# First modulation by pairs of shift and scale, gate and up beside it, angles moved into the feed-forward

## Chip, cores and metric

The kernel runs on one core of a Trainium2 chip. The metric is the time of one execution on the device in microseconds (us), as the median of some runs. Engines: TensorE (PE) multiplies matrices, with its weight loads shown as PEld; VectorE (DVE) and ScalarE (ACT) work elementwise; GpSimd (POOL) and SyncE (SP) here mainly issue loads. Each engine runs its own list of instructions in order and waits on semaphores. SBUF is the memory beside the engines, PSUM the eight banks that PE writes.

## The reference, cut to what matters

Two transformer blocks of two layers each act on x of 256 tokens by 1024 features in f32. What matters here is the very beginning of the first block, for layer 0:

```python
c_act = jax.nn.silu(c)
mod = (c_act @ ada_w[l] + ada_b[l]).reshape(bsz, N_SUB, 3, D_MODEL)[:, :, :, None, :]
h = modulate(x, norm_pre[l, 0], mod[:, 0, 0], mod[:, 0, 1])   # rms_norm(x) * gain * (1 + scale) + shift
x = residual_add(x, swiglu(h, ffn_w_gate[l, 0], ffn_w_up[l, 0], ffn_w_down[l, 0]), norm_post[l, 0], mod[:, 0, 2], 0.5)
```

The comment sums up `modulate` and is not in the code. A swiglu is `(silu(h @ w_gate) * (h @ w_up)) @ w_down` with an inner width of 2816. Much later, the second block turns queries and keys by the cosine and sine of angles made from `positions_2`.

## The kernel before, in words

**Feature-major h.** h is held as eight pieces of 128 features by 256 tokens (`hx`, with a high half `hhi` and a low half `hlo`, since PE multiplies f32 split into two parts). A piece m needs shift m and scale m, each a vector of 128. One "unit" of the modulation is 128 of those numbers: a 128x1024 slice of `ada_w` (512 KB), multiplied by silu(c) and summed along its rows on DVE (`tensor_tensor_reduce`, L2210). Units 0 to 7 are the shifts and 8 to 15 the scales of the first sublayer. They are loaded from SP's queue (L420 to L429) and from ACT's (L1524 to L1528), into buffers that other parts use later (`first_ada`, L384 to L389); the last three go into buffers that the first units have left. DVE takes them in the order 0 to 15 (L2208). Each counts up `first_used`.

**Weights.** All weight matrices pass as tiles of 128x2048 f32 (1 MB) through a ring of three slots `raw`. ACT copies a tile to its high half (`split_high`, L1224, into `whi`), DVE subtracts for the low half (`split_low`, L1811, into `wlo`), and SP loads the slot again when the low half is done (L439). In a feed-forward the tiles come as gate 0, up 0, gate 1, up 1, down 0, gate 2, up 2, down 1 and so on: tile 0 is the first gate, tile 4 the first down, tile 7 the second down.

**The opening.** DVE first makes the angles of the second block from the positions (L2182 to L2206, some fifteen small operations, a cosine part and a sine part); ACT takes their sine (L1533). DVE then runs the sixteen units, with the low half of tile 0 after the sixth. POOL loads x when the load of unit 3 has landed (L2524); ACT makes the sums of squares of x and scales its rows (L1537 to L1547); PE transposes them (`turn_rows`, L643) into banks 6, 7, 0 and 1. When all sixteen units are done, DVE adds bias and norm (`shift_scale`, L1833), ACT writes the pieces (`sublayer_begin`, L1343), DVE makes their low halves (L1930) and counts `h_ready`, and PE multiplies gate piece by piece (`features_fresh`, L863), then up in one go (`features_wide`, L874).

**The feed-forward's step on DVE** (`gate_up`, L2136): low half of the next tile, sum of the two gate banks (L2140), a modulation unit for later sublayers (L1830, from `adat`, which POOL refills as units are used, L2535), low half of the next tile, sum of the up banks (L2144), product with silu and its split (L2147 to L2154), another unit. ACT copies bank parts (L1502, L1507) and makes the silu. PE waits in `gate_up` (L887) for the sums of the chunk before and in `down` (L895) for the tile's low half and for `a_ready`.

`keep_busy` (L638) issues products of constants that nothing uses.

## Time and profile before

| | us |
|---|---|
| median of 3 runs (2280.01 to 2280.69) | 2280.08 |
| the profiled execution | 2280.72 |
| its span | 2279.1 |
| PE busy | 2217.8 (97%) |
| DVE busy | 1625.4 (71%) |
| ACT busy | 1234.0 (54%) |
| bytes moved by DMA | 467.27 MB, mean 205 GB/s |

Times in the views are counted from the start of the span. A row of the timeline names an engine, a line of the kernel, the operation, the tile written and those read, and how many such instructions were merged; in brackets stands how long the engine was idle before it and what released it. A "landing" is the time from the issue of a load to its semaphore.

### The profile page before, as it was taken

To read this page: it belongs to the slowest core of one execution; us is meant where nothing else is said; L and a number is where in the kernel's file an instruction comes from. 1 tells how busy PE (TensorE), PEld (TensorE's weight loads), DVE (VectorE), ACT (ScalarE), POOL (GpSimd) and SP (SyncE) were. 2 spreads that over 40 slices of the span, in tenths; PEclk is the share of its full clock that TensorE was granted. 3 is DMA by queue.
4 is the path that set the end of the run, shared out by engine and by line. 5 is a ranking of instruction groups with operands and counts; after the bars stand their busy time and mean duration, and the time that the engine had idled before them with its cause. 6 is when DMAs were issued, how large, how long until landed. Compare 5 with 4: busy or idle time off the path is not lost.

```text
span 2279.1 us, 37401 instructions
## 1 busy us (share of the span) xinstructions
PE 2217.8 (97%) x14332; PEld 1983.1 (87%) x14332; DVE 1625.4 (71%) x2303; ACT 1234.0 (54%) x1721; POOL 77.0 (3%) x143
## 2 busy tenths in 40 slices
PE   3999999999999999999999999999999999999998
PEld 3888989988888888899988899889888998898887
DVE  7888777677778888777686667656656667566665
ACT  4445567564455446585554465655544556565444
POOL 0100000000000010000000000000000000000000
PEclk9999999999999999999999999999999999999999
DMA  8877564547666875655565546334555464344553
GB/s 344 311 277 266 190 229 163 194 178 282 242 236 244 298 272 189 229 181 199 194 222 193 191 160 212 130 142 157 199 187 189 157 234 139 131 165 176 198 189 111
DMA packets 79506, 467.27 MB, mean 205 GB/s; under 512 B 10080, under 2 KB 10800, under 8 KB 33168
## 3 DMA queue, kind: packets, MB, share of 16 engines
q1 hardware_dynamic: 58480, 389.38, 47.6%
q0 software_dynamic: 19312, 71.74, 8.8%
q10 hardware_dynamic: 1584, 4.36, 0.5%
q8 instruction: 89, 1.46, 0.3%
q14 instruction: 41, 0.34, 0.0%
HBM read 458.56 MB, written 1.05 MB: 202 GB/s over the span
## 4 chain that ended last, share of the span: by engine, by line
PE 90%; ACT 4%; DVE 2%; issue 1%; DMA 1%; ACTq 1%; DVEq 0%
PE ps L855 21%; PE ps L860 11%; PE ps L548 11%; PE ps L525 10%; PE ps L526 10%; PE ps L527 10%; PE ps L554 5%; PE ps L809 3%; PE ps L816 2%; PE ps L685 1%; PE ps L699 1%; PE ps L732 1%; DVE wlo L1815 1%; PE ps L651 1%; DMA raw<-in_ada 1%
## 5 line engine op out<-in xcount | busy, mean ns | idle before, releaser
L1815 DVE TENSOR_TENSOR wlo<-raw,whi 128x2048 fp32r<-128x2048 f32 x360 | 824.0, 2291 | 204.1 <-ACT whi L1231 190.8
L1231 ACT ACTIVATE whi<-raw 128x2048 fp32r<-128x2048 f32 x359 | 686.8, 1914 | 244.1 <-PE ps L527 195.5
L855 PE MATMUL ps<-hx,whi 128*128 128x512 f32 x2112 | 513.8, 391 | 0.1
L855 PEld LDWEIGHTS ps<-hx,whi 128*128 128x128 f32 x2112 | 392.0, 188 | 79.9 <-issue 0.6
L860 PE MATMUL ps<-hx,wlo 128*128 128x256 f32 x2112 | 288.5, 283 | 0.0
L860 PEld LDWEIGHTS ps<-hx,wlo 128*128 128x128 f32 x2112 | 276.8, 191 | 9.8
L548 PE MATMUL ps<-hx,whi 128*128 128x256 f32 x2176 | 276.6, 285 | 3.4 <-ACT set_a L1251 3.4
L548 PEld LDWEIGHTS ps<-hx,whi 128*128 128x128 f32 x2176 | 265.5, 191 | 6.7 <-issue 6.2
L525 PE MATMUL ps<-whi,yhi 128*128 128x512 f32 (+1 forms) x560 | 215.6, 385 | 0.0
L526 PE MATMUL ps<-wlo,yhi 128*128 128x512 f32 (+1 forms) x560 | 215.1, 384 | 0.0
L527 PE MATMUL ps<-whi,ylo 128*128 128x512 f32 (+1 forms) x560 | 214.4, 383 | 0.0
L1502 ACT ACTIVATE set_b<-ps 128x512 f32<-128x512 f32 x66 | 39.6, 600 | 220.8 <-PE ps L860 220.8
L1830 DVE CUSTOM_DVE_ANT_0 adat<-adat,cact 128x1024 f32<-128x1024 f32 x128 | 155.3, 1220 | 3.7 <-DMA adat<-in_ada 3.1
L554 PE MATMUL ps<-hx,wlo 128*128 128x256 f32 x1088 | 141.5, 283 | 0.0
L554 PEld LDWEIGHTS ps<-hx,wlo 128*128 128x128 f32 x1088 | 135.5, 192 | 0.0
L1507 ACT ACTIVATE set_b<-ps 128x512 f32<-128x512 f32 x66 | 39.5, 598 | 155.4 <-PE ps L860 155.4
L527 PEld LDWEIGHTS ps<-whi,ylo 128*128 128x128 f32 x560 | 105.2, 188 | 21.1
L525 PEld LDWEIGHTS ps<-whi,yhi 128*128 128x128 f32 x560 | 105.4, 188 | 18.9
L526 PEld LDWEIGHTS ps<-wlo,yhi 128*128 128x128 f32 x560 | 105.4, 188 | 18.2
L525 PE MATMUL ps<-whi,hx 128*128 128x512 f32 (+1 forms) x320 | 119.7, 374 | 1.3 <-DVE wlo L1815 0.7
L527 PE MATMUL ps<-whi,hx 128*128 128x512 f32 (+1 forms) x320 | 117.9, 368 | 0.0
L526 PE MATMUL ps<-wlo,hx 128*128 128x512 f32 (+1 forms) x320 | 117.8, 368 | 0.0
(281 smaller groups left out, 3002.6 us busy)
## 6 DMA issues: line engine op xcount, KB each, us to landing
raw<-in_w SPq DMA_DIRECT2D x360, 1024.0 KB, 4.9
adat<-in_ada POOLq DMA_DIRECT2D x128, 512.0 KB, 4.7
blk<-in_block POOLq DMA_DIRECT2D x2, 926.5 KB, 7.4
raw<-in_ada SPq DMA_DIRECT2D x3, 512.0 KB, 9.9
set_b<-in_ada SPq DMA_DIRECT2D x3, 512.0 KB, 11.6
raw<-in_ada ACTq DMA_DIRECT2D x3, 512.0 KB, 13.1
set_a<-set_b SPq DMA_DIRECT2D x24, 64.0 KB
x<-in_x POOLq DMA_DIRECT2D x1, 1024.0 KB, 10.2
```

Source lines behind the costliest of these rows:

```text
L525: mm(out_ap, sh, mh, start=start and first, stop=False, skip_group_check=skip)
L526: mm(out_ap, sh, ml, start=False, stop=False, skip_group_check=skip)
L527: last = mm(out_ap, sl, mh, start=False, stop=stop and end, skip_group_check=skip)
L548: mm(ps[:, bank, i * S:(i + 1) * S], whi[:, slot, col:col + P], h[:, k, :], start=(i == 0 and k == 0 and h is hhi), stop=False, skip_group ...
L554: last = mm(ps[:, bank, i * S:(i + 1) * S], wlo[:, slot, col:col + P], hhi[:, k, :], start=False, stop=(k == KD - 1), skip_group_check=True)
L809: mm(out_ap, whi[:, slot, kk * 512 + i * P:kk * 512 + (i + 1) * P], y[:, n % 2, kk, :], start=(i % 2 == 0 and kk == 0 and y is yhi), stop= ...
L816: last = mm(ps[:, bank + i // 2, (i % 2) * S:(i % 2 + 1) * S], wlo[:, slot, kk * 512 + i * P:kk * 512 + (i + 1) * P], yhi[:, n % 2, kk, :] ...
L855: mm(ps[:, bank + i, :].rearrange("p (a s) -> p a s", a=2), whi[:, slot, k * 256 + i * P:k * 256 + (i + 1) * P], hx[:, :, k, :], start=fir ...
L860: return mm(ps[:, bank + i, 0:S], wlo[:, slot, k * 256 + i * P:k * 256 + (i + 1) * P], hhi[:, k, :], start=False, stop=end)
L1231: A(whi[:, slot, :], raw[:, slot, :], ACT.Copy).then_inc(*T.counts("hi_ready"))
L1815: tt(wlo[:, slot, :], raw[:, slot, :], whi[:, slot, :].bitcast(F32), ALU.subtract)\
L1830: nc.vector.tensor_tensor_reduce(adat[:, slot, :], adat[:, slot, :], cact[:, :], 1.0, 0.0, ALU.mult, ALU.add, out_ap).then_inc(*T.counts(" ...
```

## The change

- The units are taken in the order shift 0, scale 0, shift 1, scale 1, and so on (`first_unit`). Their buffers change; three units use `raw` slots 0 and 2, so tile 0 is loaded when four units are used and tile 2 when six are; tile 1 is loaded from ACT's queue among the units. The load of positions goes last. x is loaded when the second unit has landed.
- ACT loads the table for silu ahead of its wait. The squares of x are two operations of 128x1024 in place of four, with one root for both.
- The transposes go to banks 0 to 3. `first_pieces` on ACT makes shift and scale of one piece from its two units (two 128x1 operations), then writes both f32 and high half of that piece; DVE makes the low half (`first_low`), between its units. The high half of tile 1 stands between pieces 3 and 4, DVE's low half of tile 1 after unit 13 of the new order.
- `first_gate_up` on PE multiplies pieces into gate and up side by side as they come.
- DVE's first gate sum stands ahead of the low half of tile 2 (`fresh`).
- The angles are made inside the first feed-forward, one half after each of the first two chunks (`beside`), and their sine on ACT behind the loop (`sines`).

The diff, cut to its core:

```diff
@@ -260,6 +260,7 @@
         H_BANK = (6, 7, 0, 1)
+        FIRST_H_BANK = (0, 1, 2, 3)
...
@@ -381,12 +384,15 @@
-        first_ada = [raw[:, 1 + i // 2, (i % 2) * D:(i % 2 + 1) * D] for i in range(4)]
+        first_ada = [set_a[:, 8:12, :].rearrange("p a s -> p (a s)"), set_a[:, 12:16, :].rearrange("p a s -> p (a s)")]
+        first_ada += [raw[:, j, i * D:(i + 1) * D] for j in (0, 2) for i in range(2)]
         first_ada += [t.rearrange("p a s -> p (a s)") for t in
-                      (set_b[:, 0:4, :], set_b[:, 4:8, :], set_b[:, 8:12, :], set_a[:, 16:20, :],
-                       merged[:, 0:4, :], merged[:, 4:8, :], ff[:, :, :])]
-        first_ada += [adat[:, 0, :], adat[:, 1, :]]
-        first_ada += [first_ada[2], first_ada[3], first_ada[4]]
+                      (set_b[:, 0:4, :], set_b[:, 4:8, :], set_b[:, 8:12, :], set_a[:, 0:4, :], set_a[:, 4:8, :],
+                       set_a[:, 16:20, :], ff[:, :, :])]
+        first_ada += [adat[:, 0, :], adat[:, 1, :], blk[:, 0:D]]
+        def first_unit(i):
+            return i // 2 + 8 * (i % 2)
@@ -418,15 +424,13 @@
             sp.dma_start(cact[:, :], cin.partition_broadcast(P)).then_inc(s_c, 16)
-            sp.dma_start(raw[:, 0, :], w[0]).then_inc(sems["raw_full0"], 16)
-            for i in (2, 4, 6, 8, 10, 12):
-                sp.dma_start(first_ada[i], ada[i]).then_inc(s_first[i], 16)
-            for i in (13, 14, 15):
-                sp.wait_ge(sems["first_used"], i - 10)
-                sp.dma_start(first_ada[i], ada[i]).then_inc(s_first[i], 16)
-            for j, used in ((1, 2), (2, 15)):
-                sp.wait_ge(sems["first_used"], used)
-                sp.dma_start(raw[:, j, :], w[j]).then_inc(sems[f"raw_full{j}"], 16)
+            for i in range(0, 16, 2):
+                if i == 6:
+                    sp.wait_ge(sems["first_used"], 4)
+                    sp.dma_start(raw[:, 0, :], w[0]).then_inc(sems["raw_full0"], 16)
+                sp.dma_start(first_ada[i], ada[first_unit(i)]).then_inc(s_first[i], 16)
+            sp.wait_ge(sems["first_used"], 6)
+            sp.dma_start(raw[:, 2, :], w[2]).then_inc(sems["raw_full2"], 16)
@@ -640,7 +644,7 @@
-            def turn_rows():
+            def turn_rows(banks=H_BANK):
...
@@ -892,6 +896,47 @@
+            def first_gate_up():
+                T.n["g_chunks"] += 1
+                fresh_h[0] = False
+                gate, up = (4, 0), (6, 1)
+                def wides(to, k):
+                    for i in range(2):
+                        wide(*to, k, i, k == 0)
+                def narrows(to, k):
+                    for i in range(2):
+                        last = narrow(*to, k, i, k == KD - 1)
+                    return last
+                pe.wait_ge(*T.nth("hi_ready", 1))
+                for k in range(4):
+                    pe.wait_ge(*T.next("h_ready"))
+                    wides(gate, k)
+                pe.wait_ge(*T.next("lo_ready"))
+                for k in range(4):
+                    narrows(gate, k)
+                pe.wait_ge(*T.nth("hi_ready", 2))
+                for k in range(4):
+                    wides(up, k)
+                pe.wait_ge(*T.next("lo_ready"))
+                for k in range(4):
+                    narrows(up, k)
+                for k in range(4, KD):
+                    pe.wait_ge(*T.next("h_ready"))
+                    wides(gate, k)
+                    last = narrows(gate, k)
+                    if k < 6:
+                        wides(up, k)
+                        narrows(up, k)
+                last.then_inc(*T.counts("tile_used"))
+                for k in range(6, KD):
+                    wides(up, k)
+                    last = narrows(up, k)
+                last.then_inc(*T.counts("tile_used"))
@@ -907,8 +952,11 @@
-            def ffn(gate=None, more=True):
-                gate_up()
+            def ffn(gate=None, more=True, first=False):
+                if first:
+                    first_gate_up()
+                else:
+                    gate_up()
@@ -927,13 +975,12 @@
             pe.wait_ge(s_idle, 1)
-            turn_rows()
-            pe.wait_ge(sems["first_used"], 16)
-            keep_busy(8, 2)
+            turn_rows(FIRST_H_BANK)
+            keep_busy(20, 7)
...
                     fresh_h[0] = True
-                    ffn(0)
+                    ffn(0, first=layer == 0)
@@ -1354,6 +1401,27 @@
+            def first_pieces():
+                T.n["mods_ready"] += 1
+                act.wait_ge(s_base, 1)
+                for m in range(KD):
+                    if m == 4:
+                        act.wait_ge(sems["raw_full1"], 16)
+                        A(whi[:, 1, :], raw[:, 1, :], ACT.Copy).then_inc(sems["hi_ready"], 1)
+                    act.wait_ge(sems["first_used"], 2 * m + 2)
+                    A(modf[:, 0, m:m + 1], modc[:, 0, m:m + 1], ACT.Identity, bias=p1(0, "ada_b", m, 1))
+                    A(modf[:, 0, 8 + m:9 + m], modc[:, 0, 8 + m:9 + m], ACT.Identity,
+                      scale=p1(0, "norm_pre", m, 1), bias=gate_b[:, m:m + 1])
+                    act.drain()
+                    if m % 2 == 0:
+                        act.wait_ge(*T.next("tr_ready"))
+                    src = ps[:, FIRST_H_BANK[m // 2], m % 2 * S:(m % 2 + 1) * S]
+                    for dst in (h32, hhi):
+                        last = A(dst[:, m, :], src, ACT.Identity, scale=modf[:, 0, 8 + m:9 + m],
+                                 bias=modf[:, 0, m:m + 1])
+                    last.then_inc(*T.counts("t2_ready"))
...
@@ -1513,6 +1581,9 @@
                         tile_done(False)
+                if sines:
+                    act.wait_ge(sems["ang_ready"], 1)
+                    A(tables2[:, :, :], tables2[:, :, :], ACT.Sin).then_inc(sems["tab_ready"], 1)
@@ -1521,40 +1592,43 @@
-            act.dma_start(pos_in, posin.partition_broadcast(P)).then_inc(s_pos, 16)
-            act.dma_start(const[:, N_MATRICES:], const_in[:, N_MATRICES:]).then_inc(s_pos, 16)
+            act.dma_start(first_ada[1], ada[first_unit(1)]).then_inc(s_first[1], 16)
+            act.dma_start(first_ada[3], ada[first_unit(3)]).then_inc(s_first[3], 16)
+            act.dma_start(const[:, N_MATRICES:], const_in[:, N_MATRICES:]).then_inc(s_eps, 16)
             act.dma_start(const[:, 0:N_MATRICES], const_in[:, 0:N_MATRICES]).then_inc(s_const, 16)
-            for i in (0, 1, 3, 5, 7, 9, 11):
-                act.dma_start(first_ada[i], ada[i]).then_inc(s_first[i], 16)
-            act.wait_ge(s_pos, 32)
+            act.preload_act_table_set("silu_and_others")
...
             A(cact[:, :], cact[:, :], ACT.Silu).then_inc(*T.counts("c_ready"))
-            act.wait_ge(*T.next("ang_ready"))
-            A(tables2[:, :, :], tables2[:, :, :], ACT.Sin).then_inc(*T.counts("tab_ready"))
+            for i in range(5, 16, 2):
+                if i == 11:
+                    act.dma_start(raw[:, 1, :], w[1]).then_inc(sems["raw_full1"], 16)
+                act.dma_start(first_ada[i], ada[first_unit(i)]).then_inc(s_first[i], 16)
+            act.dma_start(pos_in, posin.partition_broadcast(P)).then_inc(s_pos, 16)
             use_ln_exp()
-            split_high()
+            act.wait_ge(s_eps, 16)
             act.wait_ge(s_x, 16)
-            for t, c_ in ((0, 0), (1, 0), (0, 1), (1, 1)):
-                add_square(x[:, t, side(c_)], t, c_, x_sums)
-                if c_ == 0:
-                    first_half(x_sums, t, 2 + t)
-                if (t, c_) == (0, 1):
-                    row_root(x_sums, 0, 2, r_x, T.counts("x_rms"))
-            row_root(x_sums, 1, 3, r_x, T.counts("x_rms"))
+            act.wait_ge(sems["first_used"], 2)
+            for t in range(2):
+                A(unit_x[:, t, :], x[:, t, :], ACT.Square, accum_out=x_sums[:, t, 0:1])
+            act.drain()
+            A(r_x[:, :], x_sums[:, :, 0], ACT.Ln, bias=c("eps"), scale=1.0 / D)
+            act.drain()
+            A(r_x[:, :], r_x[:, :], ACT.Exp, scale=-0.5)
...
                     .then_inc(*T.counts("u1_ready" if (t, c_) == (1, 0) else "u_ready"))
+            split_high()
...
                 with T.layer(LAYER1):
-                    sublayer_begin(modf[:, 0, 8:16], modf[:, 0, 0:8])
                     if layer == 0:
-                        act.wait_ge(sems["raw_full1"], 16)
-                        A(whi[:, 1, :], raw[:, 1, :], ACT.Copy).then_inc(sems["hi_ready"], 1)
-                    ffn(False)
+                        first_pieces()
+                    else:
+                        sublayer_begin(modf[:, 0, 8:16], modf[:, 0, 0:8])
+                    ffn(False, sines=layer == 0)
...
@@ -2133,11 +2207,14 @@
-                def gate_up(own=None):
+                def gate_up(own=None, fresh=False):
                     v.drain()
-                    tile_done(False)
+                    if not fresh:
+                        tile_done(False)
...
                     tt(gate_sum, gate_sum, ps[:, 4:6, 0:S], ALU.add).then_inc(*T.counts("ga_ready"))
+                    if fresh:
+                        tile_done(False)
@@ -2154,12 +2231,14 @@
-                gate_up(own_gate)
+                gate_up(own_gate, fresh)
...
                 ada(0)
+                beside(0)
...
                 tile_done(False)
+                beside(1)
@@ -2179,14 +2258,18 @@
-            v.wait_ge(s_pos, 32)
             posf, ang, kf = bufA[:, 0, 0:S], bufA[:, 1, 0:S], bufB[:, 0, 0:S]
-            nc.vector.tensor_copy(posf, pos_in[:, :])
-            v.drain()
-            ts(ang, posf, c("invf"), None, ALU.mult)
-            v.drain()
-            for i, quarter in enumerate((0.25, 0.0)):
-                ts(kf, ang, 1.0 / (2 * math.pi), quarter, ALU.mult, ALU.add)
+            def angles(i):
+                if i == 0:
+                    v.wait_ge(s_eps, 16)
+                    v.wait_ge(s_pos, 16)
+                    nc.vector.tensor_copy(posf, pos_in[:, :])
+                    v.drain()
+                    ts(ang, posf, c("invf"), None, ALU.mult)
+                    v.drain()
+                ts(kf, ang, 1.0 / (2 * math.pi), 0.0 if i else 0.25, ALU.mult, ALU.add)
@@ -2203,28 +2286,51 @@
                 last = ts(r, r, -3.1415925, 3.1415925, ALU.max, ALU.min)
-            last.then_inc(*T.counts("ang_ready"))
+                if i == 1:
+                    last.then_inc(sems["ang_ready"], 1)
             v.wait_ge(*T.next("c_ready"))
-            for i in range(16):
-                v.wait_ge(s_first[i], 16)
-                nc.vector.tensor_tensor_reduce(first_ada[i], first_ada[i], cact[:, :], 1.0, 0.0, ALU.mult, ALU.add,
-                                               modc[:, 0, i:i + 1]).then_inc(*T.counts("first_used"))
-                if i == 5:
-                    split_low()
-            T.n["x_rms"] += 2
+            def first(*units):
+                for i in units:
+                    u = first_unit(i)
+                    v.wait_ge(s_first[i], 16)
+                    nc.vector.tensor_tensor_reduce(first_ada[i], first_ada[i], cact[:, :], 1.0, 0.0, ALU.mult, ALU.add,
+                                                   modc[:, 0, u:u + 1]).then_inc(sems["first_used"], 1)
+            def first_low(*pieces):
+                for m in pieces:
+                    v.wait_ge(*T.next("t2_ready"))
+                    tt(hlo[:, m, :], h32[:, m, :], hhi[:, m, :].bitcast(F32), ALU.subtract)\
+                        .then_inc(*T.counts("h_ready"))
+            first(0, 1)
+            v.wait_ge(s_load, 16 * N_LOADS)
+            stt(out=gate_b[:, 0:8], in0=p1(0, "ada_b", 8, 8), scalar=1.0, in1=p1(0, "norm_pre", 0, 8),
+                op0=ALU.add, op1=ALU.mult).then_inc(s_base, 1)
+            first(2, 3, 4, 5, 6, 7, 8, 9)
+            split_low()
             T.n["u_ready"] += 3
-            v.wait_ge(s_load, 16 * N_LOADS)
...
                     if layer == 0:
-                        shift_scale(0, 0)
                         new_gain()
-                    sublayer_begin()
+                        first_low(0)
+                        first(10, 11)
+                        first_low(1, 2, 3)
+                        first(12, 13)
+                        split_low()
+                        first_low(4, 5)
+                        first(14, 15)
+                        first_low(6, 7)
+                    else:
+                        sublayer_begin()
                     ts(gate_b[:, 0:24], p1(layer, "b_gate"), 0.5, None, ALU.mult)
-                    ffn(ada_units=3, after=lambda: (gate_of(layer, 0, 0.5), new_gate(), shift_scale(layer, 1), new_gain()))
+                    ffn(ada_units=3, after=lambda: (gate_of(layer, 0, 0.5), new_gate(), shift_scale(layer, 1), new_gain()),
+                        beside=angles if layer == 0 else lambda i: None, fresh=layer == 0)
...
@@ -2521,7 +2627,7 @@
             g.dma_start(norms2_all[:, :], norms2_in[:, 0:16 * DEPTH]).then_inc(s_load, 16)
-            g.wait_ge(s_first[3], 16)
+            g.wait_ge(s_first[1], 16)
```

## Rows read from the trace of the kernel before

**Rows 1.** The page's slices of the span: busy tenths of PE and of DVE.
```profile
PE   3999999999999999999999999999999999999998
...
DVE  7888777677778888777686667656656667566665
```

**Rows 2.** Timeline of PE: start us, us, engine, line, operation, count [idle before].
```profile
34.80 3.65 PE L651 MATMUL ps<-const,set_a 128*128 128x128 f32 x16 [34.80 <-ACT set_a L1546]
38.10 2.05 PE L641 MATMUL ps<-idle 128*128 128x256 f32 x8
39.95 0.75 PE L855 MATMUL ps<-hx,whi 128*128 128x512 f32 x1
...
40.71 0.41 PE L855 MATMUL ps<-hx,whi 128*128 128x512 f32 x1
...
51.51 3.82 PE L855 MATMUL ps<-hx,whi 128*128 128x512 f32 x16
...
62.64 0.40 PE L525 MATMUL ps<-whi,yhi 128*128 128x512 f32 x1
...
79.22 0.40 PE L525 MATMUL ps<-whi,yhi 128*128 128x512 f32 x1
```

**Rows 3.** Windows: length, busy PE, PEld, DVE, ACT, POOL, granted clock, DMA.
```profile
50.00:60.00 10.00, 10.00 (x59) 8.86 (x59) 8.98 (x14) 6.28 (x6) 1.06 (x2) 1.00 0.92 349
```

**Rows 4.** Timeline of DVE in the opening.
```profile
9.10 0.29 DVE L2184 CAST bufA<-bufC 128x256 f32<-128x256 int32 x1 [9.10 <-DMA const<-in_const]
...
12.74 0.29 DVE L2189 TENSOR_SCALAR bufB<-bufA 128x256 f32<-128x256 f32 x1
...
15.61 1.22 DVE L2210 CUSTOM_DVE_ANT_0 raw<-raw,cact 128x1024 f32<-128x1024 f32 x1
...
35.43 1.22 DVE L2210 CUSTOM_DVE_ANT_0 raw<-raw,cact 128x1024 f32<-128x1024 f32 x1
...
36.58 1.22 DVE L2210 CUSTOM_DVE_ANT_0 set_b<-set_b,cact 128x1024 f32<-128x1024 f32 x1
...
43.55 0.43 DVE L1943 TENSOR_TENSOR hx<-merged,hx 128x256 fp32r<-128x256 f32 x1 [0.28 <-ACT hx L1354]
```

**Rows 5.** Timeline of DVE in the first feed-forward.
```profile
50.02 0.68 DVE L2140 TENSOR_TENSOR set_b<-set_b,ps 128x512 f32<-128x512 f32 x1
...
60.15 2.29 DVE L1815 TENSOR_TENSOR wlo<-raw,whi 128x2048 fp32r<-128x2048 f32 x1
62.36 0.68 DVE L2140 TENSOR_TENSOR set_b<-set_b,ps 128x512 f32<-128x512 f32 x1
...
74.33 2.29 DVE L1815 TENSOR_TENSOR wlo<-raw,whi 128x2048 fp32r<-128x2048 f32 x1 [0.38 <-issue]
```

**Rows 6.** DMA view of 0 to 60: GB/s in forty slices of 1.5 us.
```profile
GB/s 0 157 255 380 383 391 414 407 421 404 407 418 404 412 412 415 423 404 407 404 432 429 257 5 0 197 431 431 401 412 418 428 83 393 410 399 382 229 371 259
```

**Rows 7.** DMA view of 23 to 26 by queue (POOL's q0, ACT's q10): packets, MB.
```profile
q0 software_dynamic: 78, 0.64, 52.9%
...
q10 hardware_dynamic: 73, 0.29, 23.6%
```

**Rows 8.** DMA issues at 19.1, 36.7 and 38.1: size, us to landing.
```profile
x<-in_x POOLq DMA_DIRECT2D x1, 1024.0 KB, 10.2
...
raw<-in_w SPq DMA_DIRECT2D x1, 1024.0 KB, 4.8
...
adat<-in_ada POOLq DMA_DIRECT2D x1, 512.0 KB, 7.1
```

**Rows 9.** Timeline of ACT.
```profile
30.08 0.29 ACT L1292 ACTIVATE part<-x_sums,const 128x1 f32<-128x1 f32 x1
...
42.90 0.62 ACT L1354 ACTIVATE hx<-ps,modf 128x256 fp32r<-128x256 f32 x1
...
46.96 0.65 ACT L1502 ACTIVATE set_b<-ps 128x512 f32<-128x512 f32 x1
```

**Rows 10.** Timeline of PE, 1501 to 1503: its longest wait after the opening.
```profile
1501.98 1.19 PE L548 MATMUL ps<-hx,whi 128*128 128x256 f32 x8 [1.71 <-ACT set_a L1251]
```

More of the change, by code:

```diff
@@ L291, in build @@
         s_c = ctx.enter_context(nc.semaphore("s_c"))
+        s_eps = ctx.enter_context(nc.semaphore("s_eps"))
+        s_base = ctx.enter_context(nc.semaphore("s_base"))
         s_idle = ctx.enter_context(nc.semaphore("s_idle"))
@@ L650, in turn_rows @@
                             at = (m % 2) * S + t * P
-                            last = nc.tensor.transpose(ps[:, H_BANK[m // 2], at:at + P],
+                            last = nc.tensor.transpose(ps[:, banks[m // 2], at:at + P],
                                                        unit_x[:, t, m * P:(m + 1) * P], ident)
@@ L1495, in last_tile_done, with ffn @@
                     split_ahead()
-            def ffn(plain, more=True):
+            def ffn(plain, more=True, sines=False):
                 def gate_up():
@@ L2105, in last_tile_done, with ffn @@
                     split_low()
-            def ffn(ada_units=0, after=lambda: None, more=True, plain=False, own_gate=None):
+            def ffn(ada_units=0, after=lambda: None, more=True, plain=False, own_gate=None, beside=lambda i: None, fresh=False):
                 chunk = [0]
@@ L2338, in _ @@
                     ffn(ada_units=2 if more else 0, after=last_gate, own_gate=18)
-            v.wait_ge(*T.next("tab_ready"))
+            v.wait_ge(sems["tab_ready"], 1)
             cos2, sin2 = tables2[:, 0, :], tables2[:, 1, :]
```

## The prediction

> **What bounds the kernel now.** I read the page first. Its slices show TensorE (PE) at nine tenths or more in every slice but the first and the last, with VectorE (DVE) at seven or eight tenths in the early ones [rows 1]. So a microsecond is won or lost only where PE waits, and for this change that is the opening. The PE timeline comes next: the first transpose stands at 34.80, the first gate product of h at 39.95, and from there PE is given no idle gap: the second gate/up pair begins at 51.51, the first down product at 62.64, the second down at 79.22 [rows 2]. Everything the change can give is an earlier 62.64 and 79.22. The window 50 to 60 says who is next: DVE is busy 8.98 of 10 us beside a full PE [rows 3]. So the third view is DVE's own timeline: angles from 9.10 to 15.61, then sixteen units, last h piece at 43.55 [rows 4], then in the feed-forward the low half (wlo) of tile 4 from 60.15 to 62.36 [rows 5]. Tile 4 is the first down tile; PE takes it at 62.64. Already before, DVE delivers it 0.28 us ahead of need. That is the point on which the change turns.
>
> **How much data comes before h.** The DMA rates of the first 60 us stand near 410 GB/s from about 7.5 us to 33 us [rows 6]: the loads are a fixed bill. I count bytes. The queues share by packets, not bytes: in the window 23 to 26 the queue of x moved 78 packets and 0.64 MB, ACT's queue of units 73 packets and 0.29 MB, so x travels in packets of 8 KB and a unit in 4 KB ones [rows 7]. A tile has the same 8 KB rows as x, so I give it two thirds beside a stream of units. A load started at an idle time lands 4.8 us later for 1 MB, of which 1.05/0.41 = 2.6 is data; x took 10.2, and an adat load from POOL's queue 7.1 [rows 8].
>
> **The change, opening, by DVE.** The angles leave the opening. Units 0 and 1 lead their queues, so c and unit 1 land near 5.4, units 0 and 3 near 8.6 (1.05 MB each way through the rates of [rows 6]). DVE starts at 8.6 in place of 15.61. A unit is 1.15 us from start to start (35.43 to 36.58 [rows 4]). It then starves: unit 2 lands at 12.2, unit 4 at 15.1, unit 5 at 16.4. SP waits until four units are used (14.5) before it issues tile 0, and units 6, 8, ... stand behind that wait. They flow from 16.2. Tile 0 beside unit 7 needs 1.57 MB, to 20.1; units 6 and 9, to 22.7; unit 8 beside tile 1, to 26.3. As a test: bytes ahead of unit 8 are 9.4 MB, and the rates of before reach that at 26.1. The last units land at 34.
>
> From 26.3 DVE is never starved of units, and its own list decides: eight units (9.2), two low halves of tiles at 2.2 (60.15 to 62.36 [rows 5]), six low pieces of h at 0.35 to 0.42 (2.2): 15.9, so unit 15 is done at 42.2. Then ScalarE (ACT): two 128x1 operations, 0.20 apart and 0.29 long, and two 128x256 at 0.45 apart and 0.61 long [rows 9], about 1.7 with the drain, and DVE's piece of 0.43. **The last piece of h comes at 44.5; before it started at 43.55 and ended at 43.98.** The 7 us that the angles free are eaten by the wait for units and by wlo of tile 1, which now stands before the last piece. x is no bound: issued after unit 1, at 5.5, it lands before 15.7 at its old 10.2; the transposes follow by 21, and ACT has done pieces 0 to 3 and the high half of tile 1 by 30.
>
> PE gains all the same. It takes pieces as they come, from 31.4, gate and up side by side, and after the last piece owes one gate and two up pieces, 12 products or 2.1 us. Gate ends at 45.2, up at 46.6, against 51.51. That is 4.9 us of lead. A pace of pieces slower than this is covered until 52.9, where DVE first asks for up. The keep_busy of 20 ends before piece 0 and costs nothing.
>
> **The feed-forward, by DVE again.** ACT makes the high half of tile 2 from 44.0 to 45.8 and takes the gate bank in 0.65; in before this ended at 47.61 [rows 9]. DVE's first sum (L2140) starts at 46.5. In before it stood at 50.02, and wlo of tile 4 at 60.15: 10.13 us later [rows 5]. Now two things are added to that stretch: wlo of tile 2, moved behind the sum (2.2), and the first half of the angles with pos, 9.10 to 12.74 and a drain, 3.75 [rows 4]. So wlo of tile 4 starts at 46.5 + 10.1 + 2.2 + 3.75 = 62.6 and ends at 64.8. Down starts at 64.9 in place of 62.64: **+2.3**. PE by itself would be there at 46.6 + 0.5 for the gate sum + 11.1 (51.51 to 62.64) + 0.7 for the up sum = 58.9 to 59.2, so it stands idle for some 5.8 us. That is the whole lead given back.
>
> Next is tile 7, the second down tile. From wlo of tile 4 to wlo of tile 7 was 14.18 (60.15 to 74.33 [rows 5]); the second half of the angles adds 12.74 to 15.61 and a drain, 2.95. It starts at 79.7 and ends at 81.9, where PE needs it at 64.9 + 16.58 = 81.5. So +2.7 there. Behind it DVE has slack again (8.98 of 10 falls to the page's seven tenths), and neither later tiles nor the end of the sublayer wait. ACT's sine in the loop's wake costs 0.63 and a table load of 1.28 twice, inside ACT idle time before the gate bank; I take nothing. Angles after DVE's unit: its adat load, issued at 42.3, lands at 49.4 by the 7.1 of before [rows 8], as DVE reaches it; no cost, 0.6 either way. Removed and hidden: five copies of h (L1941), the modulation's two small sums, now on ACT.
>
> **The price of the idle 5.8 us.** PE's products in the opening of before are slow first: 8 of them in 2.05 at 38.10, and the first of 512 columns 0.75 against 0.41 for the one at 40.71 [rows 2]. The granted clock reads 1.00 in the window 50 to 60 [rows 3]; yet by the durations the pace before 40.71 was about half, as at the 1.2 GHz level. Idle had been 34.8 us; slow time was 5.9 us from the first transpose, 2.6 from the dense work at 38.10. The other end is a wait of 1.71 us at 1501.98, after which eight products of 256 columns take 1.19, the full pace [rows 10]. No gap between stands in the trace. The cost lies between 0 and half of 5.9, 2.95; I take half of 2.6, **1.3**, since down is dense work as at 38.10, and keep both ends. This bill falls behind 64.9: down 2 would start at 81.5 + 1.3 = 82.8, which covers DVE's 81.9. Against 79.22 and rounded up for the small waits: **+3.7 us**.
>
> The Trainium skill ("TensorE: Matmul & The Clock Gate", Part 1: The HAM clock gate) says that the array's clock falls to 1.2 GHz after idle time and returns only under sustained work, and that a kernel should not let PE stand for several microseconds. It speaks against this change, since the pieces and the wait for tile 4 make such a gap. Taken alone it would make the slow pace certain, rival one below.
>
> **Result of the sum.** The profiled execution took 2280.72, span 2279.1 and 1.6 around it. It becomes 2284.4. The median of the runs shown is 0.64 lower, so I predict **2283.8**. Differences under 0.2%, 4.56 us, count as no change: about what a measurement of this kernel can tell.
>
> **Rivals.**
> 1. Slower by more than 0.2%: PE falls to half pace in the gap and stays there 5.9 us. Price 2.95 in place of 1.3, so +5.4, 2285.5 (2284.7 to 2286.5). It decides if the gap before the first down is long enough for the fall; for it, the slow products after 34.8 us of idle; against it, the full pace after 1.71.
> 2. Full pace kept: +2.7, 2282.8.
> 3. The lead survives. If DVE were not starved between 17.6 and 26.3, h would end 6 us sooner, wlo of tile 4 at 59, and PE would start down at 59.2: -3.4, 2276.7. Half of that gives 2280. Against it stand the bytes: unit 8 cannot land before 26 unless others come later. Faster by over 0.2% needs down before 58.1, where PE itself is not ready.
> 4. The change doesn't do what it says: loads land later than by fair packets (small const packets ahead of unit 5, a late tile 0), unit 8 at 28.5. Each microsecond there goes straight through: +5.7, 2285.8.
>
> **How the numbers follow.** Forecast 0.45 (own range 2282.3 to 2285.2), rival one 0.17, rival two 0.18, rival three 0.10, rival four 0.10. The range leaves out the full lead of rival three and the far ends of one and four: 2280.0 to 2286.6. Slower: rival one's 0.16, rival four's 0.09, and a tail of 0.05 of the forecast, 0.30. Faster: 0.05. Same: 0.65.
>
> **What would show it.** DVE idle before units 6 and 8; unit 15 done near 42; last low piece near 44.5; L2140 first near 46.5; wlo of tile 4 ending near 64.8 with PE idle 5 to 6 us in front of the first down product, released by DVE; the first down products at 0.46 apart if the pace fell, 0.23 if not; no PE gap after 85. I am wrong if units come so early that wlo of tile 4 ends by 62, or if PE waits again in the third chunk.

## The result, and the profile after

| us | before | after |
|---|---|---|
| median (7 runs of each) | 2280.33 | 2288.14 |
| lowest to highest | 2280.01 to 2281.24 | 2286.65 to 2289.45 |
| profiled execution, its span | 2280.72, 2279.1 | 2288.19, 2286.4 |
| first gate product of h | 39.95 | 33.94 |
| second gate/up pair | 51.51 | 49.98 |
| first down product | 62.64 | 67.25 |
| second down block | 79.22 | 86.50 |

The ratio of after to before is 1.0034, with a 95% interval of 1.0024 to 1.0044: slower by 7.8 us, where +3.7 was forecast and 2286.6 was the upper end of the range. The spans differ by 7.3, and so do the starts of the second down block (7.28). All of the loss lies before 87 us, as the steps said; its size was wrong.

DVE of after, rows of the timeline (start, length, engine, line, operation, tiles, count, [idle before, releaser]), to be read against [rows 4] and [rows 5]. L2298 is a unit, L2304 the low half of a piece of h, L2215 the gate sum, L1889 the low half of a tile.

```profile
9.73 1.23 DVE L2298 CUSTOM_DVE_ANT_0 set_a<-set_a,cact 128x1024 f32<-128x1024 f32 x1 [9.73 <-DMA set_a<-in_ada]
...
16.93 1.23 DVE L2298 CUSTOM_DVE_ANT_0 raw<-raw,cact 128x1024 f32<-128x1024 f32 x1
...
26.32 1.23 DVE L2298 CUSTOM_DVE_ANT_0 set_b<-set_b,cact 128x1024 f32<-128x1024 f32 x1 [8.16 <-DMA set_b<-in_ada]
...
28.88 1.23 DVE L2298 CUSTOM_DVE_ANT_0 set_b<-set_b,cact 128x1024 f32<-128x1024 f32 x1 [0.18 <-DMA set_b<-in_ada]
...
43.32 1.22 DVE L2298 CUSTOM_DVE_ANT_0 blk<-blk,cact 128x1024 f32<-128x1024 f32 x1
...
46.27 0.43 DVE L2304 TENSOR_TENSOR hx<-merged,hx 128x256 fp32r<-128x256 f32 x1 [1.40 <-ACT hx L1421]
...
49.23 0.69 DVE L2215 TENSOR_TENSOR set_b<-set_b,ps 128x512 f32<-128x512 f32 x1 [2.45 <-ACT set_b L1570]
...
61.13 0.29 DVE L2268 CAST bufA<-bufC 128x256 f32<-128x256 int32 x1
...
64.91 2.29 DVE L1889 TENSOR_TENSOR wlo<-raw,whi 128x2048 fp32r<-128x2048 f32 x1
...
81.81 2.29 DVE L1889 TENSOR_TENSOR wlo<-raw,whi 128x2048 fp32r<-128x2048 f32 x1 [0.38 <-issue]
```

DVE works on unit 5 at 16.93 and then stands 8.16 us until unit 6 is there. From 61.13 the first half of the angles stands in front of the low half of tile 4 (64.91), the tile that the first down product needs. PE of the same trace, beside [rows 2]:

```profile
33.94 1.19 PE L859 MATMUL ps<-hx,whi 128*128 128x512 f32 x2 [7.38 <-DVE hx L2304]
36.48 2.93 PE L859 MATMUL ps<-hx,whi 128*128 128x512 f32 x6 [1.35 <-DVE hx L2304]
39.20 1.91 PE L864 MATMUL ps<-hx,wlo 128*128 128x256 f32 x8
40.91 2.52 PE L859 MATMUL ps<-hx,whi 128*128 128x512 f32 x8
...
59.89 2.07 PE L864 MATMUL ps<-hx,wlo 128*128 128x256 f32 x16
67.25 0.80 PE L529 MATMUL ps<-whi,yhi 128*128 128x512 f32 x1 [5.30 <-DVE wlo L1889]
67.85 0.63 PE L530 MATMUL ps<-wlo,yhi 128*128 128x512 f32 x1
...
72.54 0.49 PE L529 MATMUL ps<-whi,yhi 128*128 128x512 f32 x1
72.88 0.39 PE L530 MATMUL ps<-wlo,yhi 128*128 128x512 f32 x1
...
86.50 0.40 PE L529 MATMUL ps<-whi,yhi 128*128 128x512 f32 x1
```

PE stands 5.30 us in front of the first down product, released by DVE's low half, and then runs twelve products about 0.43 apart (67.25 to 72.54) before it is back at 0.23. I call this "half pace": the lower of PE's two clock levels. The windows show the same in the granted clock, the number ahead of the DMA share; columns as in [rows 3]:

```profile
40.00:50.00 10.00, 9.98 (x55) 8.63 (x53) 6.16 (x12) 5.81 (x9) 2.11 (x4) 0.90 0.66 237
50.00:60.00 10.00, 9.71 (x49) 8.18 (x50) 9.53 (x11) 7.63 (x7) 0.60 (x2) 1.00 0.82 302
60.00:70.00 10.00, 4.70 (x24) 3.92 (x23) 9.08 (x17) 2.17 (x3) 1.47 (x3) 0.80 0.56 182
70.00:80.00 10.00, 10.00 (x44) 8.31 (x43) 9.29 (x16) 2.66 (x2) 0.65 (x2) 0.86 0.83 302
```

Why did unit 6 come only at 26.3? SP issued tile 0 at 14.51, as soon as the fourth unit was used, and unit 6 at 14.88, as forecast. The landings and the queues tell the rest: SP's issues of 14.5 to 15 (size, us to landing), then packets, MB and share of the engines' time in 14.5 to 18 (q1 is SP's queue, q10 ACT's):

```profile
raw<-in_w SPq DMA_DIRECT2D x1, 1024.0 KB, 8.9
set_b<-in_ada SPq DMA_DIRECT2D x1, 512.0 KB, 11.4
```

```profile
q10 hardware_dynamic: 367, 1.35, 95.8%
q0 software_dynamic: 25, 0.07, 5.4%
q1 hardware_dynamic: 4, 0.00, 0.1%
```

In the 3.5 us after the issue of tile 0 SP's queue moved 4 packets, and none of them after 16. No bandwidth was lost: ACT's queue moved 1.35 MB in that time. What landed from it was the large constants (15.9), unit 5 (16.9) and unit 7 (18.2); of these DVE could use unit 5 at once, and unit 7 only behind unit 6. From 18 to 20 SP's queue had 66 packets beside ACT's 74.

### The profile page after: what moved, and what is told of

It reads as the page before. It is cut to its first block, busy times and chain, and to the rows that moved or that the text cites. A ratio compares the mean times of both kernels' runs of the same rounds, so it can differ in the third digit from the quotient of the medians.

```text
span 2286.4 us, 37430 instructions
## 1 busy us (share of the span) xinstructions
PE 2225.9 (97%) x14344; PEld 1988.7 (87%) x14344; DVE 1623.0 (71%) x2297; ACT 1238.5 (54%) x1734; POOL 75.5 (3%) x143
## 4 chain that ended last, share of the span: by engine, by line
PE 89%; ACT 3%; DVE 3%; issue 1%; DMA 1%; ACTq 1%; DVEq 1%; SPq 0%; POOLq 0%
PE ps L859 21%; PE ps L864 11%; PE ps L552 11%; PE ps L529 10%; PE ps L530 10%; PE ps L531 10%; PE ps L558 5%; PE ps L813 3%; PE ps L820 2%; PE ps L689 1%; PE ps L703 1%; DVE wlo L1889 1%; PE ps L736 1%; ACT whi L1278 1%; DMA set_b<-in_ada 1%
## 5 line engine op out<-in xcount | busy, mean ns | idle before, releaser
L1889 DVE TENSOR_TENSOR wlo<-raw,whi 128x2048 fp32r<-128x2048 f32 x360 | 823.6, 2290 | 204.9 <-ACT whi L1278 192.2
```

Of the source, the lines that this page charges most:

```text
L1889: tt(wlo[:, slot, :], raw[:, slot, :], whi[:, slot, :].bitcast(F32), ALU.subtract)\
```

## The experiments

Times are medians; the ratio is to the kernel before on the same chip (its medians there: 2280.25 to 2280.55). Where a profiled execution lies more than 0.7 us from its median, the text says so. Theory A, held at the start: the late unit 6, the angles in front of tile 4 and the half pace after PE's wait add up to the whole loss. Rivals: the pieces themselves cost, or one of the three is hidden by another.

**1. The half pace.** After, plus thrown-away products before the first down product.

```diff
+                if first:
+                    keep_busy(44, 0)
```

> The changed kernel with 44 products of constants, used by nothing, on PE between the second gate and up and the first down; at full pace they last 5.3 us and end with the gap. Theory A (12 products of the first down ran at 0.43 in place of 0.23 from start to start because PE had stood idle for 5.3 us, a price of 2.8 us): wlo of tile 4 ends at 67.1 as before, the first down product starts at 67.1 to 67.4 and all of them run at 0.23; the time is 2285.3. Rival B (the slow products come from something else, such as reads of the fresh tile): they stay slow and the time stays at 2288.1, or grows where the products of constants end late.

Measured: 2285.49, ratio 1.0024 (1.0014 to 1.0034). PE and the window 60 to 70:

```profile
61.45 5.43 PE L645 MATMUL ps<-idle 128*128 128x256 f32 x44
66.73 0.50 PE L529 MATMUL ps<-whi,yhi 128*128 128x512 f32 x1
67.07 0.39 PE L530 MATMUL ps<-wlo,yhi 128*128 128x512 f32 x1
```

```profile
60.00:70.00 10.00, 10.00 (x72) 9.40 (x71) 9.07 (x17) 2.69 (x3) 1.25 (x3) 1.00 0.51 184
```

The first down product comes 0.5 us earlier (DVE was ahead by that), its products stand 0.23 apart, the granted clock is 1.00, and the second down block starts at 83.64: 16.91 behind the first, where after had 19.25. So the half pace costs 2.3 us by this distance and 2.6 by the first down block alone (5.58 us long, 8.14 in after). The medians moved 2.65, with DVE's 0.5 in it. My first figure for the half pace was 1.3.

**2. The angles alone.** The kernel before with nothing but its angles moved into the feed-forward, and their sine behind the loop, as in the change.

```diff
                 ada(0)
+                beside(0)
...
+                beside(1)
```

> The kernel before, with one part of the change alone: the angles on DVE go into the first feed-forward, one half after each of the first two chunks, and the sine on ACT behind the loop. Theory A (in the old opening the angles lay beside the wait for units, so taking them out gives nothing, and in the feed-forward they stand in front of tiles 4 and 7): unit 15 is still done near 37.7, wlo of tile 4 ends at 66.1 in place of 64.65 or 62.36, the second down starts 4.0 us late, the time is 2284.3; if PE's gap of 3.5 us is enough for the slow clock, up to 2286.5. Rival B (the angles held up the opening): unit 15 done by 34, h up to 3.5 us earlier, and the time within 1 us of 2280.3.

Measured: 2284.69, ratio 1.0021 (1.0011 to 1.003). DVE and PE, in this kernel's lines:

```profile
62.35 2.29 DVE L1816 TENSOR_TENSOR wlo<-raw,whi 128x2048 fp32r<-128x2048 f32 x1
```

```profile
64.69 0.80 PE L525 MATMUL ps<-whi,yhi 128*128 128x512 f32 x1 [3.01 <-DVE wlo L1816]
```

Moving the angles costs 4.4 us by itself. The opening gets back only 0.8 us (last piece of h at 42.75, from 43.55): the first unit starts at 13.46 in place of 15.61, and then units wait for their loads. The low half of tile 4 is 2.2 later than in [rows 5]. The wait of 3.01 us is followed by products 0.43 apart until 70.4, a down block of 8.43 us.

This trace is not a typical execution. It took 2287.19, 2.5 above the median; only one other of the ten was as long (2287.30), and these two have a mean granted clock of 0.997, where seven of the other eight have 0.999, as the kernel before has. So the 4.4 us by the medians are for the most part the angles' own price, and the half pace of this trace was, as far as the clocks tell, not paid in full in most executions. The same trace lost 1.3 us more between 1340 and 1364, with a granted clock of 0.79 from 1338 to 1346 behind waits of 0.86 and 0.77 us that the kernel before has too, without a fall.

**3. The order on SP's queue.** After, with tile 0 (and the wait ahead of it) behind unit 8.

```diff
-                if i == 6:
+                if i == 10:
```

> The changed kernel, but SP issues units 6 and 8 before it waits for the fourth used unit and loads tile 0. Theory A (the wait at SP and tile 0 in front of units 6 and 8 make DVE starve, and this costs about 2 us of the last piece of h): unit 6 is taken at 18 to 19 in place of 26.3; then tile 0 comes later, near 25.7, the low half of tile 0 has to wait for its high half until about 27.7, and ACT's pieces follow at 1.55 us each, so most of the gain is lost again: last piece of h 1 to 3 us earlier, wlo of tile 4 ending at 64.3 to 66, time 2285.3 to 2287. Rival B (the fixed bill of bytes decides, in whatever order): the last piece and the time stay within 1 us. Rival C (the starving is the whole cost): last piece near 39, time under 2282.

Measured: 2283.49, ratio 1.0014 (1.0005 to 1.0024), 1.8 us below the lower end expected (the profiled execution 2284.46). The queues in 14.5 to 18 and DVE at unit 8:

```profile
q1 hardware_dynamic: 197, 0.72, 51.1%
q10 hardware_dynamic: 189, 0.64, 46.2%
q0 software_dynamic: 22, 0.05, 3.7%
```

```profile
21.17 1.23 DVE L2298 CUSTOM_DVE_ANT_0 set_b<-set_b,cact 128x1024 f32<-128x1024 f32 x1 [0.36 <-DMA set_b<-in_ada]
```

With its loads already queued SP's queue has its half. Unit 8 comes 7.7 us earlier, the last piece of h at 42.51 and the low half of tile 4 at 61.01, both 3.8 to 3.9 earlier; PE still waits 4.97 us and still falls to half pace. So the place of tile 0 and its wait are worth 4.65 us by the medians, 3.73 by the start of the second down block. Beside experiment 2, which has the angles' move and nothing else, the rest of the change costs 3.45 us by the medians in its own order (2.3 by the second down block). With tile 0 moved it no longer costs: 1.2 us less by the medians, 1.5 by the second down block, which is not clear of noise, since the runs of the two kernels overlap (2282.75 to 2285.86 and 2283.44 to 2287.30). I had not seen that the placing of one tile load decides whether the pieces cost. Whether the silent 3.5 us or the tile's own bytes carry more of the 4.65 was not told apart.

**4. The angles where DVE stands.** After, with both halves between units 5 and 6, and the positions loaded ahead of unit 5.

```diff
-            first(2, 3, 4, 5, 6, 7, 8, 9)
+            first(2, 3, 4, 5)
+            angles(0)
+            angles(1)
+            first(6, 7, 8, 9)
```

> The changed kernel, but both halves of the angles stand in the opening, between DVE's units 5 and 6 of the new order, where DVE was idle for 8.16 us; positions are loaded ahead of unit 5. Nothing else differs. Theory A (DVE's list in front of the first down tile sets the time, and the angles are 3.75 us of it): wlo of tile 4 ends 3.7 us earlier, at 63.4; the gap of PE before the first down product shrinks from 5.3 to under 2 us, so its products run at 0.23 from start to start at once; the second down starts near 80.0, and the time is about 2281.2, against 2288.1. Rival B (the late units set the time, and the angles lie beside other waits): wlo of tile 4 stays within 1 us of 67.1 and the time within 1.5 us of 2288.1. Rival C (only the slow clock costs): the same as A for the time, but wlo of tile 4 would stay at 67.

Measured: 2282.72, ratio 1.0012 (1.0002 to 1.0021); the profiled execution took 2281.93, the shortest of ten. Theory A's mechanism held: the low half of tile 4 at 61.37, and PE's wait before the first down product is 1.20:

```profile
63.71 0.50 PE L529 MATMUL ps<-whi,yhi 128*128 128x512 f32 x1 [1.20 <-DVE wlo L1889]
```

Its 24 down products take 5.57 us, against 8.14 in after: no half pace. The time is 1.5 us above the expected one. DVE waits 1.25 us before unit 6 and 1.16 for a modulation matrix at 65.42; which of them makes up the 1.5, no run separates.

**5. Both edits together, and what came up next.** Experiment 3 with the first half of the angles between units 3 and 4, its positions loaded ahead of unit 5.

```diff
-            first(2, 3, 4, 5, 6, 7, 8, 9)
+            first(2, 3)
+            angles(0)
+            first(4, 5)
+            first(6, 7, 8, 9)
```

> Two edits on the changed kernel: SP's wait and tile 0 stand behind units 6 and 8, as in the run with that edit alone, and the first half of the angles stands between DVE's units 3 and 4, where DVE had two waits of 1.1 and 1.6 us and more behind; the second half stays behind the second chunk. Theory (the two prices add: 3.9 us of late units, 3.75 us of angles in front of the first down tile, and the slow clock goes with the gap): wlo of tile 4 ends at 59.5, PE's gap before the first down is 1 to 1.5 us, all its products run at 0.23, the second down starts at 76.4, and the time is 2277.5. Rival (what is taken out in one place comes back as another wait, above all the loads of tiles 2 to 4): second down at 79 or later, time 2280 or more.

Measured: 2281.14, ratio 1.0004 (0.9995 to 1.0014): the loss is gone, but the gain of 2.8 isn't there, and the second down block starts at 79.28, as the rival said. The positions landed late, so DVE waited 3.14 us for them, and the low half of tile 4 came at 59.12 with 1.19 us of wait in PE. The prices of theory A don't simply add: alone the order was worth 4.65 us and the angles 5.42, together they are worth 7.0. The half pace is not a third sum beside them: its 2.3 to 2.6 us went with the angles' part, since a wait of 1.2 us was not followed by it. Next I took the low half of tile 1 out from between the pieces, with the low up products at the end, first on this version:

```diff
                         first(12, 13)
-                        split_low()
                         first_low(4, 5)
                         first(14, 15)
                         first_low(6, 7)
+                        split_low()
```

> As the run with the order and the first half of the angles, and besides DVE makes the low half of tile 1 behind the last piece of h in place of before pieces 4 and 5, and PE takes all sixteen products of up with it at the end. Theory (after the last piece DVE was idle for 2.5 us until the gate bank was copied, and this low half fits there): last piece 2.2 us earlier, near 40.5, first gate sum 2.6 us earlier, wlo of tile 4 ending near 57; PE itself is then the bound, second down near 74, time 2275 (2274 to 2276.5). Rival (PE needs the low half of tile 1 in time, so up ends later and the gain is lost): up ends after 46.5 and the time stays at that of the run without this edit, 2277.5.

then on after alone:

> The changed kernel with one edit: DVE makes the low half of tile 1 behind the last piece of h, and PE takes the products with it at the end of up. Theory (its place in front of the last piece costs 2.2 us, and DVE's idle 2.5 us in front of the gate sum hides it there): last piece near 44.5, wlo of tile 4 ending near 64.6, still a gap of 3 us or more and 12 to 14 slow products: 2285.6. Rival (the units' landing sets the last piece): last piece within 0.5 us of 46.7, time within 1 us of 2288.1.

and, from the first of these two, with the second half of the angles between units 5 and 6:

> As the run with the late low half of tile 1 and both other edits, but the second half of the angles stands between units 5 and 6, so none is in the feed-forward. Theory: DVE is behind the landings there only by about 1.6 us and catches up 1 us of it, so the last piece comes 0.5 to 1.5 us later; tile 7 is ready 2.95 us earlier, but PE does not wait for it: within 1 us of the run with the second half in the feed-forward, 2275 to 2276.5. Rival (tile 7 is still what PE waits for at the second down): faster by 1 to 2 us.

Measured: 2282.86 (1.0013, 1.0004 to 1.0022), 2289.44 (1.0042, 1.0026 to 1.0057) and 2283.74 (1.0013, 1.0004 to 1.0023). All three missed what I expected, in the same way. The last piece of h came earlier (43.39, 44.49, 43.95, against 45.26 in experiment 5's first kernel and 46.27 in after), and DVE gave back more than that further on, at the third unit of the first chunk: the low half of tile 4 came at 61.52, 66.12 and 63.13, where experiment 5's first kernel had 59.12 and after 64.91. (The profiled executions of the first and the third took 2283.71 and 2285.20, above their medians.) DVE, then the queues and the landings of 50 to 56, of the first of the three:

```profile
59.90 1.23 DVE L1902 CUSTOM_DVE_ANT_0 adat<-adat,cact 128x1024 f32<-128x1024 f32 x1 [3.19 <-DMA adat<-in_ada]
...
61.52 2.29 DVE L1887 TENSOR_TENSOR wlo<-raw,whi 128x2048 fp32r<-128x2048 f32 x1
```

```profile
q1 hardware_dynamic: 244, 1.75, 76.9%
q0 software_dynamic: 76, 0.31, 20.1%
...
raw<-in_w SPq DMA_DIRECT2D x2, 1024.0 KB, 8.6
adat<-in_ada POOLq DMA_DIRECT2D x1, 512.0 KB, 8.5
```

The modulation matrix is asked for by POOL when its buffer has been used, lands 8.5 us later beside two tile loads, and DVE needs it with the low half of tile 4 standing behind. DVE waited 3.19, 2.11 and 3.94 us for it. The load itself had become longer: 8.5, 7.4 and 9.2 us, where it took 4.9 in experiment 5's first kernel and 5.5 in after. An earlier DVE asked for it at most 0.9 us earlier, and got it later. That it is slower because of the tile loads that it meets is read from the traces; no run changed that alone. This wait is what I had left out of all three sums.

**6. That unit behind tile 4.** From experiment 5: the third unit of the first chunk moved behind the low half of tile 4, the second half of the angles behind the loop over the later chunks with its sines behind the last gate and up, the positions loaded behind the small constants; with and without the late low half of tile 1.

```diff
-                ada(0)
+                if not fresh:
+                    ada(0)
...
+                gate_up(own_gate if own_gate is None else own_gate + 3, late=(lambda: ada(0)) if fresh else None)
```

> After, with five edits: tile 0 is asked for behind the h units, the positions behind the small constants, the first half of the angles stands between units 3 and 4, the third unit of the first chunk (with its wait for the modulation matrices) stands behind the low half of tile 4, and the second half of the angles behind the second chunk with its sines behind the last gate and up; the low half of tile 1 stands behind the last h piece. My theory: what ends last in front of the first down product is whatever stands on VectorE between the gate sum and the low half of tile 4, and nothing but the ub sum and the second unit is left there. The low half of tile 4 starts at 55 to 57.5, TensorE waits under 1 us at its first down product, the second down block starts at 74 to 77.5, and the time is 2275 to 2278.5. Rival: the wait for the modulation matrices or for a tile comes back in front of TensorE in another place (second down block at 79 or later), and the time is 2280 or more.

> The same without the late low half of tile 1. My theory: last h piece 1 to 2 us later than with it, the low half of tile 4 at 55 to 58, the second down block at 75 to 78, the time 2276 to 2279. If it is the late low half that costs (TensorE's order at the end of up, the low tile being late), this one is the faster of the two. Rival as in the other run: 2280 or more.

Measured: 2278.67 (11 runs), ratio 0.9993 (0.9984 to 1.0002), and 2279.51, 0.9998 (0.9989 to 1.0007). DVE and PE of the first:

```profile
56.79 2.29 DVE L1887 TENSOR_TENSOR wlo<-raw,whi 128x2048 fp32r<-128x2048 f32 x1
59.91 1.23 DVE L1902 CUSTOM_DVE_ANT_0 adat<-adat,cact 128x1024 f32<-128x1024 f32 x1 [0.83 <-DMA adat<-in_ada]
```

```profile
57.87 2.08 PE L864 MATMUL ps<-hx,wlo 128*128 128x256 f32 x16
59.78 0.40 PE L529 MATMUL ps<-whi,yhi 128*128 128x512 f32 x1
...
76.36 0.40 PE L529 MATMUL ps<-whi,yhi 128*128 128x512 f32 x1
```

The places came out as expected: low half of tile 4 at 56.79, no wait of PE, the second down block 2.86 us earlier than in before. The times lie 0.2 and 0.5 us above their ranges. The span is 2.1 us shorter than that of before; PE loses the rest later, 0.47 us at 215.04 among it. The first kernel is 9.5 us faster than the change; neither can be told from before with certainty.

The profiled execution of the second took 2281.23, 1.7 above its median, and shows where such a stray comes from. Both kernels have waits of 0.47 and 1.75 to 1.76 us near 215 and 227. Behind them the granted clock of 225 to 232 is 1.00 in the first kernel's trace and 0.80 in the second's.

**7. The pieces at full pace.** In that kernel PE still ran its pieces at half pace (the window 40 to 50 has a granted clock of 0.94).

```diff
+                    if k < 2:
+                        keep_busy(30 - 4 * k, 7)
                     pe.wait_ge(*T.next("h_ready"))
                     wides(gate, k)
```

> The last version but one (third unit behind tile 4, late low half of tile 1), with products that are thrown away while TensorE waits for the first pieces of h: 30 in front of the first gate product and 26 in front of the second piece's. There TensorE was idle 4.31 and 4.07 us and ran its pieces at half pace until 45. My theory: the pieces at full pace take away its backlog (the last piece's low half was ready at 43.77, the last gate product began at 45.6), so gate and up end 1 to 1.8 us earlier and, TensorE being busy from there on, all behind them: the second down block starts at 74.6 to 75.4 (76.36 without them) and the time is 2276.5 to 2278.0. Rival: the thrown-away products run at half pace themselves and hold up the pieces, or VectorE's low half of tile 4 becomes the bound; then the second down block starts at 76.3 or later and the time is 2278.5 or more.

Measured: 2279.28, ratio 0.9997 (0.9988 to 1.0006).

```profile
40.00:50.00 10.00, 8.12 (x45) 6.39 (x44) 8.18 (x11) 8.17 (x12) 2.11 (x4) 1.00 0.62 211
```

```profile
42.70 0.73 PE L859 MATMUL ps<-hx,whi 128*128 128x512 f32 x2 [0.70 <-DVE hx L2308]
...
44.52 0.73 PE L859 MATMUL ps<-hx,whi 128*128 128x512 f32 x2 [0.86 <-DVE hx L2308]
...
46.72 2.17 PE L864 MATMUL ps<-hx,wlo 128*128 128x256 f32 x16 [0.32 <-DVE wlo L1889]
...
76.43 0.40 PE L529 MATMUL ps<-whi,yhi 128*128 128x512 f32 x1
```

The clock is full, and nothing is gained: PE now waits for the last pieces and for the low half of tile 1, and the second down block stands at 76.43. The theory falls, with one reserve: in this trace the last units landed late and the last piece came at 44.04, 0.7 later than without the edit, which hides a part of what might have been won. Here half pace cost nothing that can be seen, since PE would have waited for its pieces anyway.

## Why the prediction was wrong, step by step

- **What bounds.** Right. DVE stood 0.28 us ahead of PE at tile 4, and all that was put in front of that low half went through. Experiment 2 shows it without the rest of the change.
- **Start and first units.** Right within 1.1 us: unit 0 at 9.73 for 8.6, unit 5 at 16.93 for 16.4, the wait on SP released at 14.5 as forecast.
- **The flow from 16.2.** This is the first step that failed. By fair packets from 1.7 us after the issue, tile 0 was to land at 20.1, unit 6 at 22.7, unit 8 at 26.3. Measured: 23.4, 26.3, 28.88, since SP's queue moved next to nothing before 18. The byte count that I used as a test (9.4 MB at 26.1) could not see it: the bytes came, from the other queue. It was my fourth rival (28.5), which I had given 0.10. Experiment 3 shows that the place of tile 0 and its wait do this; why the queue stayed silent is open.
- **From unit 8 to the last piece.** Right: 15.66 us for 15.9 to the end of unit 15, then 2.16 to the end of the last low piece where I had 2.3. It ended at 46.70; my 44.5 was such an end too, though the text sets it beside before's start of 43.55.
- **The lead of PE.** Wrong by 0.5 us. Gate was to end 0.7 after the last piece. It ended at 48.57, 1.9 after it: PE had run its pieces at half pace until about 42 (eight products in 2.36 from 40.91) and had a backlog. ACT took the bank at 48.60, and DVE stood 2.45 us before its gate sum, 49.23 for 46.5. I had said that pieces slower than planned were covered until DVE asks for up. That was true of up and not of gate. That the half pace made the backlog is read from this trace; no run of after without it was made.
- **From the gate sum to tile 4.** Right: 15.68 us for 16.1. So the first down product came at 67.25 for 64.9: 2.6 later by the units, 0.4 regained up to the last piece, 0.5 lost at gate, 0.4 regained up to tile 4.
- **The price of PE's wait.** This is the second step that failed. The wait was 5.30 for 5.8, but its price 2.67 (down block 8.14, against 5.47 in experiment 6) for 1.3. Both ends, 0 and 2.95, held; the value that I took was wrong. I had counted the slow time from the dense products at 38.10 [rows 2], 2.6 us. The transposes from 34.80 belonged to it: counted from the first work after standing still it was 5.9 us there and is 5.29 here (67.25 to 72.54), and half of that is the price. The Trainium skill ("TensorE: Matmul & The Clock Gate", Part 1) says that full speed returns only under sustained work; that is what the twelve slow products show.
- **Tile 7.** Right: its low half at 81.81 for 79.7, 16.90 behind that of tile 4 for 17.1, and covered by PE.
- **The sum.** The step that made the range too narrow: I priced rivals one and four as alternatives. They exclude each other in nothing. Together they give 5.7 + 1.65 = 7.35 on the profiled execution, 2288.1 less 0.64, which is 2287.4 to the measured 2288.14. (The 5.7 was itself a little low: 28.5 less 26.3 is 2.2, on top of 3.7.) Two costs on one path that have separate causes must be added up for the upper end.

## What to carry to other kernels

Count not only how many bytes lie ahead of a load but on which queue: here a wait in front of a load emptied that queue, and the other queue took its share with data that was mostly needed later. Before work is moved off an engine's idle stretch, look at which of its later products is only just in time, and what load stands behind it; in experiments 5 and 7 what was won at one place came back as the wait for the next late thing, and only experiment 6, which moved that thing too, kept it. And when a wait on PE can lead to half pace, its price belongs beside the wait in one term, with all the other late steps on that path.

## What the runs showed of the hardware that I had not expected

- A queue that had run dry beside a busy one moved 4 packets in the 3.5 us after its next issue (14.5 to 18), where the other moved 367; with loads queued up all along the two had 197 and 189. The last kernel of experiment 5 shows it once more: its modulation matrix was issued on POOL's queue at 52.24, and from 52.3 to 55 that queue moved 1 packet where SP's moved 125. The cause of the delay was not found. In [rows 8] a tile issued at an idle time landed after 4.8 us, 2.2 of it not data.
- PE's pace after a wait, with the time lost in the first down block against 5.47 us, one trace each: waits of 1.19 and 1.20 cost 0.1 (5.59 and 5.57); 3.01 cost 2.96; 3.91 cost 1.7; 4.66 cost 1.7; 4.97 cost 2.85; 5.30 cost 2.67; 6.64 cost 2.6. In these traces the price is a step, near 0, near 1.7 or 2.6 to 3.0, and it doesn't grow with the wait. The length of the wait alone doesn't decide it: in experiment 2 most executions seem to have paid less than the traced one, and in experiment 6 nearly the same short waits (0.47 and 1.75 to 1.76) were followed by a fall in one kernel's trace and not in the other's.
- A modulation matrix of 512 KB took 4.9, 5.5, 7.4, 8.5 and 9.2 us to land in five kernels of this case that asked for it within 2.6 us of each other (51.38 to 53.95), always with tile loads of SP's beside it; [rows 8] has 7.1 for one asked for at 38.1.
